# Conv block in 16 chunks of 128 channels, taps split 14 to 17, and silus moved on ScalarE

## The reference, cut to what matters

```python
def _conv_mixer(h, w_in, b_in, dw_w, dw_b, ln_g, ln_b, w_out, b_out):
    u = h @ w_in + b_in                 # 2048 -> 4096 channels
    a, gt = jnp.split(u, 2, axis=-1)
    u = a * jax.nn.sigmoid(gt)          # gated linear unit (GLU)
    u = depthwise_causal_conv(u, dw_w)  # 31 taps, one filter a channel
    u = jax.nn.silu(_layer_norm(u + dw_b, ln_g, ln_b))
    return u @ w_out + b_out
```

## Time and profile before

| | |
|---|---|
| Median of 3 runs | 2567.16 us (2566.07 to 2567.51) |
| Profiled execution | 2565.03 us, span 2563.0 us |
| Granted TensorE clock | mean 0.999 |
| Busy in the span | TensorE 2539.6 us (99%), VectorE 1865.5 us (73%), ScalarE 1280.6 us (50%), GpSimd 223.5 us (9%) |
| `conv_in` on TensorE | 1523.1 to 1725.5 us |
| Last sums of the layer norm | 1741.7 us |
| First product of `conv_out` | 1751.7 us |

### The profile page before, as it was taken

The page is one execution under the profiler, slowest core; times in us unless marked ns, Lnnn a source line. Parts: engine busy times, 40 slices in busy tenths (PEclk is TensorE's granted clock), DMA queues, the critical chain, the costliest instruction groups (busy, mean ns, idle before and its releaser), DMA issues.

```text
span 2563.0 us, 38927 instructions
## 1 busy us (share of the span) xinstructions
PE 2539.6 (99%) x14630; PEld 2197.7 (86%) x14630; DVE 1865.5 (73%) x2099; ACT 1280.6 (50%) x1672; POOL 223.5 (9%) x277
## 2 busy tenths in 40 slices
PE   8999999999999999999999999999999999999999
PEld 8888888888888898888888889997888888888887
DVE  7787657768778868887788766988787565565564
ACT  6645545544445556454455457776543343343443
POOL 2000000000000000000000005771000000000000
PEclk9999999999999999999999999999999999999999
DMA  7544446889899765778877745554676666656665
GB/s 219 169 134 121 125 123 229 287 266 321 278 316 327 273 231 175 254 261 267 289 243 261 253 150 188 166 164 162 236 250 229 200 188 194 191 180 198 188 194 167
DMA packets 291845, 555.30 MB, mean 217 GB/s; under 512 B 17185, under 2 KB 96114, under 8 KB 290674
## 3 DMA queue, kind: packets, MB, share of 16 engines
q1 hardware_dynamic: 270994, 442.06, 53.8%
q0 software_dynamic: 19072, 104.88, 12.3%
q10 hardware_dynamic: 1632, 6.29, 0.6%
HBM read 551.06 MB, written 2.11 MB: 216 GB/s over the span
## 4 chain that ended last, share of the span: by engine, by line
PE 93%; DVE 3%; ACT 2%; issue 1%; DMA 0%; POOL 0%; SPq 0%; ACTq 0%; DVEq 0%; POOLq 0%
PE sums L682 43%; PE small L682 10%; PE sums L716 9%; PE small L716 9%; PE sums L722 5%; PE small L722 5%; PE sums L739 4%; PE sums L746 2%; PE small L1818 1%; DVE w_lo L631 1%; ACT w_hi L622 1%; PE sums L1523 0%; PE small L835 0%; PE small L1484 0%; PE sums L3365 0%
## 5 line engine op out<-in xcount | busy, mean ns | idle before, releaser
L622 ACT ACTIVATE w_hi<-raw 128x1024 fp32r<-128x1024 f32 x814 | 859.6, 1060 | 1156.7 <-PE sums L682 432.7
L631 DVE TENSOR_TENSOR w_lo<-raw,w_hi 128x1024 fp32r<-128x1024 f32 x814 | 998.5, 1234 | 586.8 <-ACT w_hi L622 585.0
L682 PE MATMUL sums<-w_hi,y_hi 128*128 128x512 f32 x672 | 263.4, 392 | 2.1 <-issue 1.9
L682 PE MATMUL sums<-w_hi,y_lo 128*128 128x512 f32 x672 | 261.7, 389 | 0.0
L716 PE MATMUL sums<-x_two,w_hi 128*128 128x512 f32 x1024 | 256.9, 393 | 0.6 <-DVE x_two L1074 0.6
L716 PE MATMUL small<-x_two,w_hi 128*128 128x512 f32 x1024 | 256.4, 392 | 0.0
L682 PE MATMUL sums<-w_hi,x_two 128*128 128x512 f32 x896 | 224.1, 392 | 0.0
L716 PEld LDWEIGHTS sums<-x_two,w_hi 128*128 128x128 f32 x1024 | 184.4, 189 | 33.9 <-issue 0.7
L716 PEld LDWEIGHTS small<-x_two,w_hi 128*128 128x128 f32 x1024 | 184.2, 189 | 32.9
L1477 DVE SCALAR_TENSOR_TENSOR mod_acc<-mod_raw,cond,mod_acc 128x1536 f32<-128x1536 f32 x105 | 190.3, 1812 | 12.4 <-DMA mod_raw<-in_mod_w_dram 12.4
L682 PEld LDWEIGHTS sums<-w_hi,x_two 128*128 128x128 f32 x896 | 167.0, 188 | 35.3 <-issue 1.2
(11 more groups left out here) (455 smaller groups left out, 3634.1 us busy)
## 6 DMA issues: line engine op xcount, KB each, us to landing
raw<-in_mlp_w_dram SPq DMA_DIRECT2D x256, 512.0 KB, 4.4
raw<-in_w_in_dram SPq DMA_DIRECT2D x198, 512.0 KB, 4.5
mod_raw<-in_mod_w_dram POOLq DMA_DIRECT2D x112, 768.0 KB, 6.1
raw<-in_w_up_dram SPq DMA_DIRECT2D x128, 512.0 KB, 4.2
raw<-in_w_down_dram SPq DMA_DIRECT2D x64, 512.0 KB, 4.7
raw<-in_conv_w_in_dram SPq DMA_DIRECT2D x128, 256.0 KB, 3.9
raw<-in_w_o_dram SPq DMA_DIRECT2D x32, 512.0 KB, 6.2
raw<-in_conv_w_out_dram SPq DMA_DIRECT2D x32, 512.0 KB, 5.8
```

The source lines that it names most:

```text
L622: act.activation(w_hi[:, s.slot(k), :], raw[:, s.slot(k), :], ACT.Copy).then_inc(hi_ready, 1)
L631: dve.tensor_tensor(w_lo[:, s.slot(k), :], raw[:, s.slot(k), :], w_hi[:, s.slot(k), :].bitcast(F32), ALU.subtract).then_inc(lo_ready, 1)
L682: mm = pe.matmul(o, l, r, start=first and i == 0 and part != "lo", stop=end and part != "hi" and i + 1 == len(steps), skip_group_check=True)
```

## The change

- **16 chunks** of one block of 128 channels. A unit now holds four tile rows of 128 columns of `a` and 128 of the gate, so a chunk has four units of 512 KB. Each is loaded by four transfers of 128 KB (before: two of 256 KB), with rows of 512 bytes (before: 1 KB). The number of units, of matmuls and of bytes is the same.
- **Whole units**: the first of each four (tile rows 0 to 3), 16 of 64; before 3 of each 8, 24 of 64.
- **Taps**: GpSimd 14, VectorE 17 of 31; the products on ScalarE lie in the first three units of a chunk. The ring between holds 16 products of 128x256.
- `tap_dve` is unchanged, and with `CV_B` = 1 its wait is for the tap just before.
- `shift_pe` moves to the last unit of chunk 2. The first chunk waits for two groups of normed tiles ahead of each unit. Unit 3 of `conv_in` is now rounded among the norm's operations.
- **Layer norm**: same tiles of two; fills of 7, 0 and 13 in place of 14, 7 and 8.
- **Delta part**: a delta silu is held back until the first unit of the next piece has been rounded; the silu of the second gate moves from the first `window` piece to the first `stick` piece. At the start four roundings stand ahead of the squares of `x`, and five products of constants stand after the first turned rows.

```diff
-CV_C = 8
+CV_C = 16
 CV_B = KT // CV_C
-CV_WHOLE = (0, 3, 6)
-POOL_TAPS = 13
+CV_UNITS = 4
+CV_K = KT // CV_UNITS
+CV_WHOLE_UNITS = (0,)
+CV_WHOLE = tuple(g for g in range(KT // 2) if 2 * g // CV_K in CV_WHOLE_UNITS)
+POOL_TAPS = 14
-PRODUCTS = 8
+PRODUCTS = 16
...
-                src = w[k * UK * P:(k + 1) * UK * P, :, c * CV_B * P:(c + 1) * CV_B * P]
+                src = w[k * CV_K * P:(k + 1) * CV_K * P, :, c * CV_B * P:(c + 1) * CV_B * P]
                 slot_free(sp, s, k)
-                to = raw[:, s.slot(k), :].rearrange("p (t h n) -> p t h n", t=UK, h=2)
-                for t in range(UK):
-                    sp.dma_start(to[:, t, :, :], src[t * P:(t + 1) * P, :, :]).then_inc((raw_loaded, raw_half)[t][s.slot(k)], 16)
+                to = raw[:, s.slot(k), :].rearrange("p (t h n) -> p t h n", t=CV_K, h=2)
+                for t in range(CV_K):
+                    sp.dma_start(to[:, t, :, :], src[t * P:(t + 1) * P, :, :]).then_inc((raw_half if t else raw_loaded)[s.slot(k)],
+                                                                                        16)
...
                 if u == NF_CONV and g in CV_WHOLE:
+                    if g == 1:
+                        rest_units(dve, s, k - 1, k)
                     continue
...
             for q in range(4):
+                round_units(act, s, SLOTS + q, SLOTS + q + 1)
                 first_squares_act(act, q)
-                round_units(act, s, SLOTS + q, SLOTS + q + 1)
...
                     s = delta_spot(n, a)
-                    round_units(act, s, *ahead(s), beside)
+                    round_units(act, s, SLOTS, SLOTS + 1, beside)
+                    late_silu()
+                    round_units(act, s, SLOTS + 1, s.size + SLOTS, beside)
                     finished(s)
...
                     if a == 1 and m > 0:
-                        delta_silu(act, g, m - 1)
+                        silus.append((g, m - 1))
...
                 finished(s)
                 act.activation(win_q[:, 2 * a:2 * a + 2, :], cross_pair(s), ACT.Copy, scale=WIN_DH ** -0.5).then_inc(dn_cross, 1)
-                if a == 0:
-                    gate_silu(1)
...
                     s = spot("stick", 2 * n + a)
-                    round_units(act, s, *ahead(s), beside)
+                    round_units(act, s, SLOTS, SLOTS + 1, beside)
+                    if n + a == 0:
+                        gate_silu(1)
+                    round_units(act, s, SLOTS + 1, s.size + SLOTS, beside)
...
-                products_act(act, c - 1, POOL_TAPS * n // 7 if n < 7 else POOL_TAPS, min(POOL_TAPS * (n + 1) // 7, POOL_TAPS))
+                products_act(act, c - 1, POOL_TAPS * min(n, 3) // 3, POOL_TAPS * min(n + 1, 3) // 3)
                 round_units(act, spot("conv_in", c), k, k + 1)
...
             s = spot("conv_in", LAST)
-            rest_units(dve, s, SLOTS, s.size, lambda n: tap_dve(dve, LAST - 1, n), TAPS_ONE // 2)
-            for n in range(TAPS_ONE // 2, 2 * TAPS_ONE // 3):
+            for n in range(2 * TAPS_ONE // 3):
                 tap_dve(dve, LAST - 1, n)
             glu(LAST)
...
             turn_quarter(0)
+            for _ in range(5):
+                pe.matmul(sums[:, 1, 1, 0:P], ident[:, :], ones[:, :], start=True, stop=True)
...
+            def normed_tiles(tile, end):
+                for g in range(tile // 2, end // 2):
+                    normed_ready(pe, NF_CONV, g)
+
+            def shift_late(tile, end):
+                if end == KT:
+                    shift_pe(pe)
+
+            multiply(pe, spot("conv_in", 0), x_hi, x_lo, True, 2 * CV_B * P, before=normed_tiles, beside=beside)
+            beside.rest()
             for c in range(1, CV_C):
-                multiply(pe, spot("conv_in", c), x_hi, x_lo, True,
-                         before=(lambda tile, end: shift_pe(pe) if tile == KT // 2 else None) if c == 2 else None)
+                multiply(pe, spot("conv_in", c), x_hi, x_lo, True, 2 * CV_B * P, before=shift_late if c == 2 else None)
...
-            fill(spot("conv_out", 0), spot("conv_out", 0).reads(), 14)
+            fill(spot("conv_out", 0), spot("conv_out", 0).reads(), 7)
             spread_pe(pe, 0, ln_mean)
-            fill(spot("conv_out", 0), spot("conv_out", 0).reads(), 7)
             spread_pe(pe, 1, ln_scaled)
-            fill(spot("conv_out", 0), spot("conv_out", 0).reads(), 8)
+            fill(spot("conv_out", 0), spot("conv_out", 0).reads(), 13)
```

More of the change, by code:

```diff
@@ L212, in build_program @@
     plan.chunk += FFN_C
-    plan.whole = (plan.unit, CV_C, 8, CV_WHOLE)
-    plan.lay("conv_in", [8] * CV_C)
+    plan.whole = (plan.unit, CV_C, CV_UNITS, CV_WHOLE_UNITS)
+    plan.lay("conv_in", [CV_UNITS] * CV_C)
     plan.lay("conv_out", [8, 8], 2)
@@ L401, in build_program @@
                 cv_g = sb("cv_g", [P, CV_B, T], scope=s1)
-                cv_sq = sb("cv_sq", [P, CV_B, T], scope=s1)
+                sb("cv_after", [P, (4 - CV_B) * T + (2 - CV_B) * 2 * (TAPS - 1 + T)], scope=s1)
                 pad30 = sb("pad30", [P, 2, CV_B, TAPS - 1 + T], scope=s1)
@@ L611, in halves_loaded @@
             u = u - spot("conv_in", 0).unit if isinstance(u, int) else -1
-            if 0 <= u < 8 * CV_C:
-                eng.wait_ge(raw_half[s.slot(k)], 16 * (u // SLOTS + 1))
+            if 0 <= u < CV_UNITS * CV_C:
+                eng.wait_ge(raw_half[s.slot(k)], 16 * (CV_K - 1) * (u // SLOTS + 1))
         def round_units(act, s, first, last, beside=None):
@@ L1946, in build_program @@
         DIAG_STEP = 2
-        last_sums = sums[:, spot("conv_in", LAST).pair, 0, :]
+        last_sums = sums[:, spot("conv_in", LAST).pair, 0, 0:CV_B * T]
         def taps_pe(pe):
@@ L2021, in dve_sums @@
         def dve_sums(c):
-            return small[:, 2 + c % 2, :]
+            return small[:, 2 + c % 2, 0:CV_B * T]
         def tap_dve(dve, c, n):
@@ L2086, in spread @@
         def spread(n):
-            return small[:, 2 + n, 0:T].rearrange("p (t n) -> p t n", n=P).unsqueeze(1).to_broadcast([P, CV_B, TT, P])
+            return small[:, 2 + n, 0:T].rearrange("p (t n) -> p t n", n=P).unsqueeze(1).to_broadcast([P, 2, TT, P])
         IDENT_MADE = 3
@@ L2253, in _ @@
                 pooled(pool, c)
-            pool.wait_ge(cv_split, CV_C)
+            pool.wait_ge(cv_split, NG)
             for kt in range(KT):
@@ L2316, in _, with late_silu @@
             beside = Beside(ab_act(act, own))
+            silus = []
+            def late_silu():
+                if silus:
+                    delta_silu(act, *silus.pop())
             def gate_silu(g):
@@ L2536, in beside_unit @@
                 n = k - SLOTS
-                products_act(act, c - 1, POOL_TAPS * n // 7 if n < 7 else POOL_TAPS, min(POOL_TAPS * (n + 1) // 7, POOL_TAPS))
+                products_act(act, c - 1, POOL_TAPS * min(n, 3) // 3, POOL_TAPS * min(n + 1, 3) // 3)
                 round_units(act, spot("conv_in", c), k, k + 1)
-                if c < LAST and n % 8 in CV_WHOLE:
-                    tile = (len(CV_WHOLE) * (c - 1) + CV_WHOLE.index(n % 8)) * DIAG_STEP
+                if c < LAST and n % CV_UNITS in CV_WHOLE_UNITS:
+                    tile = (len(CV_WHOLE_UNITS) * (c - 1) + CV_WHOLE_UNITS.index(n % CV_UNITS)) * DIAG_STEP
                     diag_act(act, min(tile, CV_B * PE_TAPS_LAST), min(tile + DIAG_STEP, CV_B * PE_TAPS_LAST))
@@ L2561, in _ @@
                 for b in range(CV_B):
-                    act.activation(cv_g[:, b, :], sums[:, s.pair, 1, b * T:(b + 1) * T], ACT.Sigmoid,
+                    act.activation(cv_g[:, b, :], sums[:, s.pair, 0, (CV_B + b) * T:(CV_B + b + 1) * T], ACT.Sigmoid,
                                    bias=parm("b_in", KT + CV_B * c + b)).then_inc(cv_gated, 1)
@@ L2572, in _ @@
             act.activation(spare[:, 1:2], eps_col[:, 0:1], ACT.Silu)
-            for j in range(CV_C):
+            for j in range(NG):
                 act.wait_ge(ln_normed, j + 1)
-                y = slice(CV_B * j, CV_B * (j + 1))
-                for b in range(CV_B * j, CV_B * (j + 1)):
+                y = slice(2 * j, 2 * (j + 1))
+                for b in range(2 * j, 2 * (j + 1)):
                     o = cv[:, b, :, 0:P]
@@ L2579, in _ @@
                 own.wait()
-                act.activation(by_tile(y_hi[:, y, :]), cv_tiles(CV_B * j, CV_B), ACT.Copy).then_inc(ln_silu, 1)
+                act.activation(by_tile(y_hi[:, y, :]), cv_tiles(2 * j, 2), ACT.Copy).then_inc(ln_silu, 1)
                 if OUT_ROUND <= j < OUT_ROUND + SLOTS:
@@ L3024, in centred @@
             def centred(j):
-                o = cv_tiles(CV_B * j, CV_B)
+                o = cv_tiles(2 * j, 2)
                 dve.tensor_tensor(o, o, spread(0), ALU.subtract).then_inc(ln_centred, 1)
             def normed(j):
-                o = cv_tiles(CV_B * j, CV_B)
+                o = cv_tiles(2 * j, 2)
                 dve.wait_ge(ln_centred, j + 1)
@@ L3036, in _ @@
             normed(0)
-            for j in range(CV_C):
```

(15 more changed lines are left out.)

## The result

The changed kernel takes 2575.24 us (median of 7 runs, 2574.09 to 2577.63) against 2566.07 for the kernel before on the same chip (7 runs, 2563.44 to 2568.72): ratio 1.0039, 95% interval 1.0028 to 1.0050. It is 9.2 us slower. The forecast was 2571 in 2556 to 2585, with the largest chance, 0.41, on slower. The profiled execution took 2576.70 us, its span 2575.1 (before 2565.03 and 2563.0).

What follows compares the result with a forecast made beforehand. TensorE bounds the kernel before; in the changed conv block VectorE's dependent taps were to bind. 2565.0 - 1.2 - 5.2 + 13.5 - 2.8 = 2569.3, plus 2.1 for the median: 2571 us, range 2556 to 2585.

Steps and rivals of the forecast that it cites:

- Steps 6 and 7: Delta part, -5.2 us from moved silus, and start, -1.2 us from five products of constants: shorter TensorE waits, clock kept.
- Step 5: Layer norm: with 7 fills the broadcast follows at once, -2.6 us, and half the last sums another -0.2: -2.8.
- Step 3: Start of `conv_in`: chunk 0 ends at 1538.9, 3.7 us later than at full rate; chunk 1's GLU is done at 1561.3.
- rival A: `conv_in`: waits between taps cost nothing, TensorE bounds; last sums +4.5 us, 2562.4 in all; chance 0.2.
- Step 2: VectorE in a new chunk: dependent taps step 0.52 us, not 0.39; 13.4 us against TensorE's 12.5, so VectorE becomes the bound.
- B: Rival: taps' waits cost nothing and TensorE's last taps halve from 13 to 6.5 us: 2552; chance 0.1.
- GpSimd: 14 adds of half size: GpSimd in a conv chunk: adds of 0.71 us, 9.9 of 13.4 us, hidden; from 0.96 they bind.
- rival C: GpSimd's add has a large fixed part and decides from 0.96 us; at 1.1 a chunk is 15.4 us: 2600; chance 0.1.
- The 13 chunks: VectorE's chain in `conv_in`: 13 chunks of 13.4 us to chunk 14's GLU, plus 1 us for late `w_hi`.
- Step 4: VectorE's chain to the end of `conv_in`: end part 18.7 us behind chunk 14's GLU, last sums starting at 1755.2.
- +13.5: Conv block: last sums start at 1755.2, where they started at 1741.71.
- Rival D: Queue of transfers, twice as many: binds from 0.84 us an issue; at 0.9, 2585; chance 0.08.

Runs made afterwards that it cites:

- e1: Kernel before with only the edits outside the conv block (delta silus, start, layer norm fills): 2555.59 us against 2565.29, ratio 0.9961.
- e8: e7 with 12 taps on GpSimd and two whole units of four a chunk in place of one, so fewer `w_lo`: 2564.96 us, ratio 0.9998.
- e2: Kernel before, each VectorE tap waiting for the tap just before it, not the one before the last: 2582.71 us, ratio 1.0070.
- e6: Changed kernel with 13 taps a chunk on GpSimd in place of 14 (VectorE 18): 2577.91 us, ratio 1.0047.
- e3: Changed kernel with VectorE's even and odd taps made independent in two PSUM halves, the join adding both: 2578.47 us, ratio 1.0055.
- e7: Changed kernel with the independent taps of e3 and 13 taps on GpSimd: 2568.89 us, ratio 1.0013.
- e5: Changed kernel with 15 taps a chunk on GpSimd in place of 14 (VectorE 16): 2587.86 us, ratio 1.0085.
- e4: Changed kernel with ScalarE's two scalings of `h` moved ahead of the sigmoids of chunks 5 and 6: 2576.05 us, ratio 1.0042.
- e9: e8 with the products for the mean placed behind chunk 2's last unit, not ahead of it: 2561.73 us, ratio 0.9987.
- e10: e9 with the scalings of `h` moved as in e4: 2560.40 us, ratio 0.9978.

## Why the prediction was right, and where it was short

The verdict, slower, and the range held; the forecast was 4 us low. As a change it had some 4 us where 9.2 were measured, and 2571 itself lies below the 2572.3 from which it called the kernel slower. Part of the nearness is luck: its sum for the profiled execution, 2569.3, was 7.4 us low (2576.70). It added 2.1 for the median, but the median of the changed kernel stands 1.5 below its profiled execution. By its steps:

- **Steps 6 and 7, -6.4: right, -7.15.** The same norm products stand at 1513.64, where they were at 1520.79. Both stretches of low clock are gone, and of the two waits before them 0.5 us, at L1842's place, is left; e1 has it without the conv block.
- **Step 5, -2.8: right, -2.6.** From the last sums to `conv_out` 10.02 us before, 7.39 after.
- **Step 3: nearly right.** GLU 1 ends at 1555.35, worked out 1561.3 - 7.15 = 1554.15. What the forecast did not price (rival A has some 3 us for it) is the wait for the mean of block 0 in chunk 2, 5.68 us, and the low clock behind it. It cost the changed kernel little, since TensorE was not the bound there; in e8, where it was, moving it gave about 3 us.
- **Step 2, VectorE's chunk: nearly right.** The tap's step is 0.52, and e2 shows its cause; `w_lo` is 1.44 reported, so some 1.35 in step; e6's 14.0 us fits the working. GLU 1 to GLU 14 take 180.27 us in 13 chunks. Less 3.5 us of waits for `w_hi` and GpSimd that is 13.6 a chunk where 13.4 was worked out. Rival A (2562) is refuted by this, B with it.
- **"GpSimd: 14 adds of half size, 0.71 us by half of 1.42 ... hidden": the step that failed.** The add steps by 0.986, past the 0.96 from which I let rival C decide, and 14 of them are 13.8 us and not 9.9. I took half of a duration as the cost of half the work, with no fixed part, and a duration as a step. From 1587.60 on GpSimd adds without a pause until 0.1 us before the last joins, so a faster VectorE alone wins nothing (e3).
- **The 13 chunks: +5.1.** 13 x 13.4 and 1.0 for late `w_hi` were worked out, 180.27 measured. VectorE's own waits divide it: 2.2 more for `w_hi`, 0.3 for GpSimd, and 2.6 are its own operations.
- **Step 4, the end part: +2.1 more.** Worked out 18.7 us, measured 20.8 from the end of GLU 14 to the last sums: the joins wait 2.04 and 0.26 us for GpSimd. TensorE's low clock in its last taps (30 in 8.72 us, 6.75 in e8) stayed hidden.

The term "+13.5" for the conv block is therefore the mis-sized one. Measured it is 1756.44 - 1741.71 + 7.15 = +21.9, and 1.2 + 5.1 + 2.1 is the 8.4 between. Two chains reach the last sums nearly together, so this is over-determined: by VectorE's waits GpSimd's part is 0.3 + 2.04 + 0.26 = 2.6 us, and e3 shows that VectorE's part can't be won back by itself. Rival C's mechanism is right and its price was too high: at 1.1 us an add it had 2600. Rival D is refuted: the queue issues a transfer in a median of 0.61 us, and it lands after 2.6.

In e3 and e7 the taps leave less time between operations and GpSimd's step rises to 1.00 and 1.006. The traces speak for the `w_lo` and against the taps as the cause: from 1598 to 1725 us, in all three kernels, about one add for each `w_lo` takes over 1 us (27 adds for 27 `w_lo` in the changed kernel, 27 for 27 in e3, 29 for 30 in e7), and every other add takes 0.64 or 0.73 us. No run takes the taps or the `w_lo` away alone. What decides between 0.64 and 0.73 stays open.

## What to carry to other kernels

When blocks are halved, price every engine's chain again, the slowest one's and the next one's. Halving gives half the elements, but all of the fixed part and of the wait for the one before, and it can turn two independent chains, taken in turns, into one dependent chain. Two engines at 13.6 and 13.8 us hide each other: a test that relieves one shows nothing (e3, e6), one that loads it more (e5) or relieves both (e7, e8) does. A wait of TensorE is worth its time only in a stretch where TensorE is the bound (e4 against e9 and e10).

## What the hardware showed

**GpSimd's step is longer than its reported duration, and beside a `w_lo` of VectorE an add takes twice as long.** The answers on the add's line, first 1540 to 1547 us in the changed kernel, then 1726.5 to 1729.5 around the `w_lo` that starts at 1727.33 (minimum, median and maximum in ns):

```profile
L2017 POOL TENSOR_TENSOR cv<-cv,cv_p x8: 719/730/736, 1539.9 to 1545.9; 128x256 f32<-128x256 f32 x8
```

```profile
L2017 POOL TENSOR_TENSOR cv<-cv,cv_p x3: 637/638/1437, 1726.4 to 1728.0; 128x256 f32<-128x256 f32 x3
```

An add of 256 columns takes 0.73 or 0.64 us, and 0.14 lie between two; beside a `w_lo` one takes 1.44, 0.8 more than its neighbours. Three `w_lo` a chunk are enough for what 13.8 us have over 14 undisturbed steps (14 x 0.83 = 11.6 us, about half of the adds being of either length). The same line of the kernel before, 1560 to 1730, has adds of 512 columns at a median of 1.19, so half the columns are 54 to 61% of the time:

```profile
L2011 POOL TENSOR_TENSOR cv<-cv,cv_p x89: 1178/1193/2063, 1559.8 to 1729.6; 128x512 f32<-128x512 f32 x89
```

The mean of 1.42 that I had halved was one of undisturbed and blocked adds. The other side pays as well: `w_lo` takes 1.22 us before `conv_in` and a median of 1.53 beside the adds. This agrees with the exclusive lock of the Trainium skill (page "SBUF — State Buffer", section "Who interferes with whom").
